# State-space scan: running sums broadcast from three bfloat16 parts, state decay on GpSimd

## The reference, cut to what matters

```python
cum = jnp.cumsum(dtc * a, axis=2)                       # running sums inside a chunk, per head
seg = cum[:, :, :, None, :] - cum[:, :, None, :, :]
decay = jnp.exp(jnp.where(tri, seg, -jnp.inf))          # t, s, head
y_intra = einsum(cb * decay, xdt)                       # inside the chunk
to_end = jnp.exp(cum[:, :, -1:, :] - cum)
states = einsum(bf, xdt * to_end[..., None])            # what the chunk adds to the state
chunk_decay = jnp.exp(cum[:, :, -1, :])
hc, h_in = hc * chunk_decay + states, hc                # one step of the recurrence
y_inter = einsum(cf * jnp.exp(cum)[..., None], h_in)    # what the state gives to the chunk
```

## Time and profile before

| | |
|---|---|
| median of 3 runs | 1339.85 us (1339.02 to 1343.07) |
| the profiled execution's own time | 1334.55 us |
| its span, first to last instruction | 1332.8 us |
| busy, PE / PE weight loads | 1195.9 us (90%) / 1058.9 us (79%) |
| busy, DVE / ACT / POOL | 703.7 us (53%) / 563.9 us (42%) / 111.3 us (8%) |
| mean granted PE clock | 0.949 |

### The profile page before, as it was taken

The page is one execution under the profiler, slowest core; times in us unless marked ns, Lnnn a source line. Parts: engine busy times, 40 slices in busy tenths (PEclk is TensorE's granted clock), DMA queues, the critical chain, the costliest instruction groups (busy, mean ns, idle before and its releaser), DMA issues.

```text
span 1332.8 us, 18238 instructions
## 1 busy us (share of the span) xinstructions
PE 1195.9 (90%) x7845; PEld 1058.9 (79%) x7845; DVE 703.7 (53%) x795; ACT 563.9 (42%) x687; POOL 111.3 (8%) x165
## 2 busy tenths in 40 slices
PE   5998999999979799999999898889769999999960
PEld 4996668999967499999899897569757777788850
DVE  5313543663269462323334723543379999888845
ACT  5324552333246342222214512421157668677832
POOL 1000211000036200000000000000010110000003
PEclk9998989999969899999999999899879999999995
DMA  8331000231300023332435621001399999999926
GB/s 265 131 107 55 1 0 16 65 96 49 88 24 2 32 56 88 80 88 88 135 94 205 202 70 64 1 16 40 115 347 344 421 385 382 354 403 379 362 96 207
DMA packets 95261, 198.30 MB, mean 149 GB/s; under 512 B 4192, under 2 KB 71928, under 8 KB 82888
## 3 DMA queue, kind: packets, MB, share of 16 engines
q1 hardware_dynamic: 86672, 167.52, 36.0%
q0 software_dynamic: 6032, 21.11, 4.4%
q10 hardware_dynamic: 2472, 8.44, 1.6%
HBM read 178.41 MB, written 18.65 MB: 148 GB/s over the span
## 4 chain that ended last, share of the span: by engine, by line
PE 68%; DVE 17%; ACT 7%; issue 3%; DMA 3%; POOL 0%; ACTq 0%; SPq 0%; POOLq 0%; DVEq 0%
PE ps L1804 44%; DVE buf_r L761 8%; PE ps L823 4%; PE ps L1903 3%; ACT buf_r L754 3%; PE ps L2003 2%; DVE buf_r L924 1%; PE ps L833 1%; PE ps L1881 1%; PE ps L2133 1%; PE ps L1917 1%; DMA buf<-y_rows,buf 1%; ACT buf_r L410 1%; DVE buf_r L414 1%; DMA buf<-in_w_in 1%
## 5 line engine op out<-in xcount | busy, mean ns | idle before, releaser
L1804 PE MATMUL ps<-buf_r,buf_r 128*128 128x288 f32 (+1 forms) x4752 | 615.0, 291 | 14.1 <-DVE buf_r L414 11.7
L1804 PEld LDWEIGHTS ps<-buf_r,buf_r 128*128 128x128 f32 x4752 | 610.2, 190 | 15.7 <-DVE buf_r L414 7.6
L404 DVE TENSOR_TENSOR buf_r<-buf,buf_r 128x2048 fp32r<-128x2048 f32 (+2 forms) x53 | 117.5, 2219 | 227.9 <-ACT buf_r L398 227.9
L761 DVE TENSOR_TENSOR buf_r<-buf,buf_r 128x2048 fp32r<-128x2048 f32 x96 | 214.1, 2283 | 1.0 <-ACT buf_r L754 1.0
L823 PE MATMUL ps<-buf_r,buf_r 128*128 128x512 f32 x768 | 188.2, 401 | 3.4 <-DVE buf_r L924 3.4
L754 ACT CAST buf_r<-buf 128x2048 fp32r<-128x2048 f32 x96 | 178.6, 1909 | 10.8 <-DMA buf<-in_w_gate_e 9.7
L823 PEld LDWEIGHTS ps<-buf_r,buf_r 128*128 128x128 f32 x768 | 144.2, 191 | 35.1 <-DVE buf_r L924 4.2
L398 ACT CAST buf_r<-buf 128x2048 fp32r<-128x2048 f32 (+2 forms) x53 | 96.6, 1823 | 127.5 <-PE ps L1804 122.2
L833 PE MATMUL ps<-buf_r,buf_r 128*128 128x512 f32 x384 | 92.4, 395 | 2.5 <-DVE buf_r L947 1.4
L833 PEld LDWEIGHTS ps<-buf_r,buf_r 128*128 128x128 f32 x384 | 71.8, 188 | 20.4 <-DVE buf_r L761 2.4
L490 ACT ACTIVATE buf<-buf 128x1024 f32<-128x1024 f32 (+1 forms) x22 | 23.2, 1056 | 84.3 <-DVE buf L1787 61.2
(11 more groups left out here) (266 smaller groups left out, 1108.5 us busy)
## 6 DMA issues: line engine op xcount, KB each, us to landing
buf<-in_w_gate_e SPq DMA_DIRECT2D x32, 1024.0 KB, 8.2
buf<-in_w_up_e SPq DMA_DIRECT2D x32, 1024.0 KB, 7.3
buf<-in_w_down_e SPq DMA_DIRECT2D x32, 1024.0 KB, 7.2
buf<-in_w_in SPq DMA_DIRECT2D x16, 1024.0 KB, 5.8
buf<-in_w_in SPq DMA_DIRECT2D x17, 512.0 KB, 5.0
buf<-in_w_mem_kv SPq DMA_DIRECT2D x8, 1024.0 KB, 5.8
y_rows<-buf ACTq DMA_DIRECT2D x16, 512.0 KB, 8.3
buf<-in_x_prompt SPq DMA_DIRECT2D x8, 512.0 KB, 5.6
```

Source lines behind the costliest of these rows:

```text
L404: nc.vector.tensor_tensor(r32(raw), raw, w_hi(n), ALU.subtract).then_inc(wl_ready, 1)
L761: nc.vector.tensor_tensor(e_lo(t), e_raw(t), e_hi(t), ALU.subtract).then_inc(wl_ready, 1)
L1804: last = nc.tensor.matmul(out, a, b, start=(k == 0 and j == 0), stop=(k == len(parts) - 1 and j == 2))
```

## The change

Two new bfloat16 tiles: CUM3 holds three parts of the running sums at partitions 0, 32 and 64 (CUM rounded, the remainder rounded, the remainder of that rounded), each on 16 partitions, zeros between them; SEL3 holds three copies of the 16x16 identity at the same partitions. A broadcast of one head is then one matmul over 80 partitions, single-pass, in place of a float32 one over 16. The parts are made by five DVE instructions, each waiting for the one before, between DIAG and the copy of CR. POOL's clearing of HS, and the first broadcast, wait for the last of the five. SEL3 and CUM3 are cleared before the convolution stage, and SEL3 is filled by three small copies.

The state's decay moves from DVE (in place) to POOL, which writes HDEC, two buffers of 128x512 in the space of the tile H0R. It stands between CE(v) and DX(v) in POOL's stream and waits for the state sum of v - 2. DVE's state sum reads HDEC and writes HS.

```diff
+        CUM3, SEL3 = A.half(TS), A.half(NH)
+        HDEC = [H0R.rearrange("p b n -> p (b n)")[:, 512 * i:512 * (i + 1)] for i in range(2)]
@@ POOL
-            pool.wait_ge(dve_dt, 7)
+            pool.wait_ge(dve_dt, 12)
             nc.gpsimd.memset(HS[:, 0], 0.0).then_inc(pads, 1)
             for v in range(10):
                 pool.wait_ge(ec_ready, v + 1)
                 nc.gpsimd.tensor_tensor(CE[v % 2], CE[v % 2], bc(XC[...]), ALU.mult).then_inc(ce_ready, 1)
+                if v == 0:
+                    pool.wait_ge(pre_dve, 5)
+                    pool.wait_ge(pre_act, 2)
+                if v >= 2:
+                    pool.wait_ge(h_ready, v - 1)
+                hs = HS[:, 0 if c < 4 else 1, g, :].rearrange("p (h q) -> p h q", h=8)
+                nc.gpsimd.tensor_tensor(HDEC[v % 2].rearrange("p (h q) -> p h q", h=8), hs,
+                                        bc(CD[:, c, 8 * g:8 * g + 8].unsqueeze(2), [P, 8, HD]), ALU.mult).then_inc(h_dec, 1)
@@ DVE, before the convolution and before dp_psum
+            nc.vector.memset(CUM3[0:80, :], 0.0)
+            nc.vector.memset(SEL3[0:80, :], 0.0).then_inc(vec_ready, 1)
+            for r in (0, 32, 64):
+                nc.vector.tensor_copy(SEL3[r:r + NH, :], IDENT[r:r + NH, r:r + NH])
@@ DVE, after DIAG
+            nc.vector.tensor_copy(CUM3[0:NH, :], CUM[0:NH, :]).then_inc(dve_dt, 1)
+            dve.wait_ge(dve_dt, 8)
+            nc.vector.tensor_tensor(DTA[32:32 + NH, :], CUM[0:NH, :], CUM3[0:NH, :], ALU.subtract).then_inc(dve_dt, 1)
+            dve.wait_ge(dve_dt, 9)
+            nc.vector.tensor_copy(CUM3[32:32 + NH, :], DTA[32:32 + NH, :]).then_inc(dve_dt, 1)
+            dve.wait_ge(dve_dt, 10)
+            nc.vector.tensor_tensor(RST[64:64 + NH, :], DTA[32:32 + NH, :], CUM3[32:32 + NH, :], ALU.subtract).then_inc(dve_dt, 1)
+            dve.wait_ge(dve_dt, 11)
+            nc.vector.tensor_copy(CUM3[64:64 + NH, :], RST[64:64 + NH, :]).then_inc(dve_dt, 1)
@@ DVE, in the scan
-                nc.vector.tensor_tensor(hs, hs, bc(CD[:, c, 8 * g:8 * g + 8].unsqueeze(2), [P, 8, HD]),
-                                        ALU.mult).then_inc(h_dec, 1)
                 dve.wait_ge(st_psum, v + 1)
                 dve.wait_ge(h_dec, v + 1)
-                nc.vector.tensor_tensor(HS[:, sq, g, :], HS[:, sq, g, :], bank(6), ALU.add).then_inc(h_ready, 1)
+                nc.vector.tensor_tensor(HS[:, sq, g, :], HDEC[v % 2], bank(6), ALU.add).then_inc(h_ready, 1)
@@ PE, ssd_first
+                elif v == 0:
+                    pe.wait_ge(dve_dt, 12)
                 for h in range(8):
-                    last = nc.tensor.matmul(cum_banks(v)[:, h, :], bc(IDENT[0:NH, 8 * g + h:8 * g + h + 1], [NH, P]), CUM[0:NH, tk],
+                    last = nc.tensor.matmul(cum_banks(v)[:, h, :], bc(SEL3[0:80, 8 * g + h:8 * g + h + 1], [80, P]), CUM3[0:80, tk],
                                             start=True, stop=True)
```

More of the change, by code:

```diff
@@ L1263, in _ @@
                     pool.wait_ge(xc_ready, CONV_C)
-                    pool.wait_ge(vec_ready, 4)
+                    pool.wait_ge(vec_ready, 5)
                 pool.wait_ge(ec_ready, v + 1)
@@ L1586, in _ @@
                 split_low(dve, n)
+            dve.wait_ge(vec_ready, 3)
+            for r in (0, 32, 64):
+                nc.vector.tensor_copy(SEL3[r:r + NH, :], IDENT[r:r + NH, r:r + NH])
             dve.wait_ge(dp_psum, 1)
@@ L1656, in _ @@
                 nc.vector.tensor_tensor(YT, bank(3).rearrange("p (j t) -> p j t", j=4), DX, ALU.add).then_inc(t3_done, 1)
-                hs = HS[:, sq, g, :].rearrange("p (h q) -> p h q", h=8)
-                nc.vector.tensor_tensor(hs, hs, bc(CD[:, c, 8 * g:8 * g + 8].unsqueeze(2), [P, 8, HD]),
-                                        ALU.mult).then_inc(h_dec, 1)
                 dve.wait_ge(st_psum, v + 1)
                 dve.wait_ge(h_dec, v + 1)
-                nc.vector.tensor_tensor(HS[:, sq, g, :], HS[:, sq, g, :], bank(6), ALU.add).then_inc(h_ready, 1)
+                nc.vector.tensor_tensor(HS[:, sq, g, :], HDEC[v % 2], bank(6), ALU.add).then_inc(h_ready, 1)
                 dve.wait_ge(t3_done, v + 1)
@@ L1955, in _ @@
                 tproj(2 * (i % 2), W_Z + i // 2, (i % 2) * P, HTH, HT).then_inc(zt_psum, 1)
-            pe.wait_ge(vec_ready, 3)
+            pe.wait_ge(vec_ready, 4)
             pe.wait_ge(ysb_ready, 5)
@@ L1977, in _ @@
             pe.wait_ge(dve_dt, 7)
-            pe.wait_ge(vec_ready, 4)
+            pe.wait_ge(vec_ready, 5)
             for c in range(NC_):
```

## The result

The changed kernel is slower: ratio to before 1.0066, 95% interval 1.0047 to 1.0085, which on 1339.85 us is +8.8 us (6.3 to 11.4). Medians of twelve runs each are 1351.15 us (1346.06 to 1355.98) and 1343.59 us (1338.39 to 1347.60). The forecast was +5.8 us within -5 to +13, slower by more than 0.3% with a chance of 0.50. The profiled execution took 1347.18 us, 12.6 more than that of before, with a span of 1345.5.

The account below looks back on a forecast made before the run. DVE's loop, with PE's nearly equal, bounds the scan now, the DVE-POOL pair afterwards; +1.7 at v = 1, +4.9 to v = 9 and -0.8 at the end add +5.8 to 1339.85, giving 1345.6 us, range 1334.5 to 1353.

Parts of the forecast that it names:

- What bounds the kernel: Scan: DVE's loop closes each 5.98 us iteration, PE's 5.94 nearly equal; neither half alone wins much, together they could.
- the exclusion: DVE instructions with two SBUF inputs and POOL instructions exclude each other; 5.67 us of such work per iteration after.
- The prices: Per scan iteration: eight new broadcasts 0.54 us for 1.98 (bounds 0.43 and 0.99), decay on POOL 1.03, CE 2.36.
- the sign of the decision: In long scan iterations POOL's CE asks 0.07 us ahead of DVE's SEG product, so CE goes first.
- The threshold of 0.61: In the scan, CE goes ahead of the SEG product if the eight broadcasts' price b is under 0.61 us.
- The start: Scan starts 2.4 us later; output matmuls of v = 0 come 2.0 earlier, those of v = 1 1.7 later.
- The iteration: Scan's output matmuls spaced 5.59 and 8.13 us by turns against 5.98; +4.9 us from v = 1 to v = 9.
- rival (2): PE's clock falls in the scan's long iterations, some 1.5 us each; +12 us, 1352 us; chance 0.23.
- The end: From v = 9's output matmuls to the state sum, the decay drops out: -0.8 us.
- The sum: Whole kernel: +1.7 at v = 1, +4.9 to v = 9, -0.8 at the end, total +5.8 us.
- Rival (1): SEG product goes first after v = 1, if broadcast price b exceeds 0.61 us; +0.3 us, 1340 us; chance 0.30.
- Rival (3): DVE and POOL exclude each other more mildly; scan's freed loop of 5.13 us runs; -10.5 us, 1329 us; chance 0.12.

Follow-up runs that it names:

- e8: Kernel before with the three-part bfloat16 broadcasts alone, decay still on DVE, plus CBM and YT in PSUM; ratio to before 0.9976.
- e9: Kernel before with only the tiles CBM and YT moved to PSUM; ratio to before 0.9987.
- e11: Changed kernel with three more, unneeded broadcasts per iteration (eleven in place of eight); ratio to before 0.9984.
- e6: Changed kernel with six extra unread float32 matmuls ahead of the output matmuls of v = 1, 3, 5 and 7; ratio to before 1.0015.
- e10: Changed kernel with the eight broadcasts of every iteration done twice; ratio to before 0.9989.
- e5: Changed kernel with CBM and YT in PSUM, so SEG and gate products on DVE have one SBUF input each; ratio to before 0.9904.
- e2: Changed kernel without the new broadcasts (float32 over 16 partitions as before), only the decay on POOL; ratio to before 0.9992.
- e7: e5 with the split's remainders in free rows of SELP, so POOL clears HS beside the split; ratio to before 0.9900.

## Why the prediction was right, and where its size was off

**What bounds the kernel.** Right as far as it was tried. With the exclusion gone, shortening PE alone left the spacing where it was (e8 and e9, both 5.92), and taking the decay off DVE as well gave 5.12, for a computed 5.13.

**The prices.** The broadcasts took 0.45 to 0.46 and not 0.54: 0.057 each, near the lower bound of 0.43, so the fixed part read off rows 5 isn't there for them. It moved CE's request further ahead, 0.13 us before the SEG product's where 0.07 had been worked out, so the sign of the decision held. The Trainium skill's 81 ns in a stream (TensorE: Matmul & The Clock Gate, section "Back-to-back issue gap") would have turned it; the trace has 57 ns. The threshold of 0.61 was a little high: 0.46 plus the 0.13 of the changed kernel and e11's 0.61 less its 0.04 put it at 0.57 to 0.59. The chosen price of 0.54 lay under it by less than its own error, so that the sign came out is in part luck. The decay on POOL took 1.05 undisturbed, DX 1.03, CE 2.36.

**The start.** Casts 0.48 (estimated 0.54), subtractions 0.82 (0.83). The first transposes came 8.08 us after the running-sum instruction's start, against 5.93: +2.15 for +2.4. The output matmuls of v = 0 at 16.46 against 18.76: -2.3 for -2.0. Those of v = 1 at 27.0 against 25.75: +1.3 for +1.7; L406 met CE and CE met SEG as laid out.

```profile
370.89 0.47 DVE L1627 CAST buf<-buf 16x640 bf16<-16x640 f32 x1
371.40 0.81 DVE L1629 TENSOR_TENSOR buf<-buf,buf 16x640 f32<-16x640 f32 x1
...
374.22 0.95 POOL L1260 MEMSET buf<- 128x1024 f32 x1 [11.03 <-DVE buf L1635]
...
375.28 1.23 DVE L1642 COPY buf<-ps 128x1024 f32<-128x1024 f32 x1 [0.76 <-POOL buf L1260]
```

**The iteration.** Long ones 8.06 for 8.13. Short ones 7.2 to 7.3 for 5.59: this is the term that was mis-sized. The layout was right, as e6 shows with 5.65 and 8.09, but it held at full clock only. That was rival (2), priced at 1.5 us for each of four iterations and given 0.23; measured are 1.6 to 1.7 each, 6.7 in all. So from v = 1 to v = 9 the scan lost 11.3 us and not 4.9, and rival (2), with its +12 us, is what the profile shows. I should have ranked it over the forecast: rows 7 had the clock down after stretches with little PE work, and none of the rows shows it kept over a wait of 3.5 us. The time fell into the range by way of this rival; the forecast's own +5.8 held for the order and not for the clock.

**The end.** 3.30 from the last output matmuls to the end of the last state sum against 4.09: -0.8, as computed.

**The sum.** +1.3 + 11.3 - 0.8 = +11.8 for the profiled scan, +8.8 (6.3 to 11.4) by the timed runs. Part of why the timed runs show less than the profiled pair is that before's profiled execution, 1334.55, is below all twelve of its timed runs. Its mean clock over the whole execution was 0.949; the 68 executions of before that were timed beside the experiments had 0.937 to 0.950, with medians of 0.943 to 0.945, and took longer where it was lower. The changed kernel's twelve had 0.935 to 0.942, the profiled one 0.941. So most executions of before lose clock somewhere that the profiled one kept it; where, a mean doesn't tell.

**Rival (1)** needed b above 0.61 and came true in e10 and e11 (+2.7 and +1.4 us for a computed +0.3). **Rival (3)**, the milder exclusion, is refuted by the changed kernel and is what e5 makes real: -10.2 for its -10.5.

## What to carry to other kernels

Before moving elementwise work to GpSimd, sum up what it and DVE would do with two SBUF operands each, and ask who will ask first: a long GpSimd instruction that gets in by 0.1 us ahead of a short critical one costs its whole length, and making an upstream step faster can be what lets it in. The cure that gave most here was a PSUM operand for the DVE instruction, where a bank allows it (1.0% under before); to hold the long instruction behind the critical one only got the loss back. Each wait of some 3.5 us on PE was paid twice here, the second time at half clock.

## What the runs showed of the hardware that I had not expected

The granted clock also came down where the profile shows PE all but fully busy. In e2 the windows read:

```profile
412.00:416.00 4.00, 4.00 (x46) 3.59 (x42) 3.24 (x5) 2.40 (x7) 4.00 (x3) 1.00 0.00 0
416.00:420.00 4.00, 3.77 (x42) 2.79 (x41) 3.49 (x7) 3.88 (x10) 2.97 (x3) 1.00 0.02 4
420.00:424.00 4.00, 3.91 (x29) 2.87 (x29) 4.00 (x7) 2.03 (x6) 2.22 (x3) 0.95 0.00 2
424.00:428.00 4.00, 4.00 (x35) 3.55 (x33) 1.97 (x4) 2.40 (x7) 3.06 (x3) 0.62 0.00 0
```

The clock went from 2.4 to 1.2 GHz near 423.6 us after stretches with 3.8 and 3.9 of 4.0 us busy. Over 396 to 440 us e2 had 43.4 of 44 us busy at a clock of 0.89, and e9 43.4 at 0.96. The kernel before had as much in the same stretch and kept 1.00:

```profile
396.00:440.00 44.00, 43.40 (x431) 34.70 (x431) 39.17 (x68) 30.80 (x78) 28.43 (x15) 1.00 0.01 1
```

And e5, e7 and e8 had PE busy only 35.4, 34.7 and 32.8 of 44 us, with gaps, and kept 1.00 too. So in these profiles the busy share doesn't say whether the clock holds. e2 and e9 differ from those three in the float32 broadcasts over 16 of 128 partitions, a third of PE's busy time, but the kernel before has the same broadcasts, so they alone don't explain it. Each is one execution; what brought the clock down in e2 and e9 isn't shown.
